# The first 18 expert picks are summed between the query tiles of a fused transformer kernel

## The reference, cut to what matters

```python
def chunk(t):
    qh = (t @ w_q).reshape(T, PEER_HEADS, 2, PEER_KEY_DIM // 2)
    s = jnp.einsum('thpd,hpnd->thpn', qh, sub_keys)
    s_top, i_top = lax.top_k(s, PEER_TOPK)
    cand = s_top[:, :, 0, :, None] + s_top[:, :, 1, None, :]
    cand_idx = i_top[:, :, 0, :, None] * PEER_N_KEYS + i_top[:, :, 1, None, :]
    best, pos = lax.top_k(cand.reshape(T, PEER_HEADS, 256), PEER_TOPK)
    idx = jnp.take_along_axis(cand_idx.reshape(...), pos, axis=-1)
    g = jax.nn.softmax(best, axis=-1)
    ue = jnp.take(u_tab, idx, axis=0)
    ve = jnp.take(v_tab, idx, axis=0)
    act = jax.nn.gelu(jnp.einsum('thkd,td->thk', ue, t), approximate=False)
    return jnp.einsum('thk,thkd->td', g * act, ve)
```

## Time and profile before

| what | value |
|---|---|
| time, median of 3 runs | 3190.19 us (3185.8 to 3191.19) |
| span of the profiled execution, first to last instruction | 3170.1 us |
| busy in the span: PE, DVE, ACT, POOL | 87%, 67%, 40%, 20% |
| mean granted TensorE clock | 0.941 of full speed |
| HBM read | 784.05 MB |
| bytes fetched by index | 536.90 MB, 73728 packets |
| indices of unit 0 ready, first fetch | 577.7, 578.75 us |
| last query tile done, first dot | 613.3, 619.17 us |

### The profile page before, as it was taken

The page is one execution under the profiler, slowest core; times in us unless marked ns, Lnnn a source line. Parts: engine busy times, 40 slices in busy tenths (PEclk is TensorE's granted clock), DMA queues, the critical chain, the costliest instruction groups (busy, mean ns, idle before and its releaser), DMA issues. The chain is left out here.

```text
span 3170.1 us, 39855 instructions
## 1 busy us (share of the span) xinstructions
PE 2755.9 (87%) x13380; PEld 2006.7 (63%) x13380; DVE 2135.5 (67%) x4563; ACT 1269.1 (40%) x2848; POOL 625.3 (20%) x531
## 2 busy tenths in 40 slices
PE   6999898887789887588888999597888997899998
PEld 6777687633344442245566777365877896778886
DVE  6784454398878876775685666855676778654445
ACT  3336523344434443465453222454543543432222
POOL 0000000244444445333332333230000001000000
PEclk9999899999999999799998999798998998899998
DMA  6531122599999999899898999883322453222221
GB/s 236 214 123 61 41 80 81 212 421 421 421 421 420 420 416 414 318 364 417 348 407 351 396 417 417 348 351 140 127 87 87 160 188 111 87 93 93 93 93 53
DMA packets 145015, 788.52 MB, mean 249 GB/s; under 512 B 15297, under 2 KB 18497, under 8 KB 79041
## 3 DMA queue, kind: packets, MB, share of 16 engines
q0 software_dynamic: 73728, 536.90, 41.4%
q1 hardware_dynamic: 65424, 229.90, 20.3%
q10 hardware_dynamic: 5680, 19.40, 1.7%
HBM read 784.05 MB, written 2.10 MB: 248 GB/s over the span
## 5 line engine op out<-in xcount | busy, mean ns | idle before, releaser
L581 POOL DMA_INDIRECT slots<-in_experts,consts x312 | 374.1, 1199 | 1189.5 <-DVE consts L2148 577.9
L2171 DVE SCALAR_TENSOR_TENSOR slots<-slots,work 128x1024 f32<-128x1024 f32 x312 | 382.1, 1225 | 93.0 <-DMA slots<-in_experts,consts 80.8
L883 PE MATMUL psum<-slots,acc 128*128 128x512 f32 x652 | 317.9, 631 | 77.0 <-ACT acc L1482 77.0
L1796 DVE TENSOR_TENSOR wlo<-w,whi 128x1024 fp32r<-128x1024 f32 x259 | 314.5, 1220 | 84.2 <-ACT whi L1277 83.5
L1277 ACT ACTIVATE whi<-w 128x1024 fp32r<-128x1024 f32 x259 | 272.3, 1053 | 215.8 <-PE psum L629 210.0
L883 PEld LDWEIGHTS psum<-slots,acc 128*128 128x128 f32 x652 | 124.8, 200 | 255.7 <-issue 131.4
L627 PE MATMUL psum<-xhi,whi 128*128 128x512 f32 x632 | 255.3, 404 | 1.9 <-DVE wlo L1796 1.9
L628 PE MATMUL psum<-xlo,whi 128*128 128x512 f32 x632 | 250.5, 396 | 0.0
L629 PE MATMUL psum<-xhi,wlo 128*128 128x512 f32 x632 | 250.5, 396 | 0.0
L1470 ACT ACTIVATE consts<-consts 128x1 f32<-128x1 f32 x512 | 101.0, 197 | 360.2 <-DVE slots L2171 215.7
L614 PE MATMUL psum<-xres,w 128*128 128x256 f32 x1040 | 238.3, 386 | 0.0
(11 more groups left out here) (358 smaller groups left out, 5829.5 us busy)
## 6 DMA issues: line engine op xcount, KB each, us to landing
w<-in_stream SPq DMA_DIRECT2D x408, 512.0 KB, 3.6
arena<-in_wmod SPq DMA_DIRECT2D x4, 2048.0 KB, 17.8
arena<-in_wmod ACTq DMA_DIRECT2D x8, 1024.0 KB, 5.5
acc<-in_wmod ACTq DMA_DIRECT2D x8, 1024.0 KB, 8.1
slots<-in_experts,consts POOLq DMA_INDIRECT x312, 17.1
split_slots<-in_experts,consts POOLq DMA_INDIRECT x148, 17.8
xres<-in_xT SPq DMA_DIRECT2D x1, 2048.0 KB, 14.8
outT<-xres SPq DMA_DIRECT2D x8, 256.0 KB, 2.0
```

The lines of the kernel that those rows point to most:

```text
L581: pool.indirect_dma_start(out=slots[slot], out_offset=None, in_=a["experts"], in_offset=bass.IndirectOffsetOnAxis(ap=indices[:, p:p + 1], ...
L883: mm = pe.matmul(bank(6 + half), diag(p), v[:, half * T:(half + 1) * T], start=(c == 0), stop=(c == PICKS - 1))
L1796: dve.tensor_tensor(wlo[:, s, :, :].rearrange("p k n -> p (k n)"), w32[:, s, :], whi[:, s, :, :].rearrange("p k n -> p (k n)").bitcast(F32 ...
L2171: dve.scalar_tensor_tensor(u, u, 1.0, tokens[:, p // PICKS, :], ALU.mult, ALU.mult, accum_out=inner[:, c:c + 1]).then_inc(sem("dotted"), 1)
```

## The change

- DVE runs the search of unit 0 through (keys, pairs, experts) with one weight split in between, and does the later splits behind it. ACT's exponential for unit 0 moves from behind the query tiles into step 7.
- Picks 0 to 17 are taken up behind query tiles 9 to 15: 3, 2, 3, 2, 3, 2, 3 of them (`SUMMED_BY`). In a step DVE does the dots ahead of its split, ACT the weights behind its copies and its split, PE the sums behind the scores.
- Until pick 22 only the six slots 4, 5, 7, 8, 10, 11 are used; the eight others open at pick 22 (`SLOTS_OPEN`).
- So that banks 6 and 7 are free for the sums, the scores of tiles 8 to 15 go to bank 4 (`key_bank`). The diagonals of the first 18 picks and the identity for turning the tokens lie in constants that are not used there; slots 10 and 11 move to offset 8192 and wait for two token copies instead of eight. All other edits are counts that follow from this. No pick below 336 is added by DVE (`on_dve`).

```diff
+QUERY_PICKS = 18
+SUMMED_BY = {9: 3, 10: 5, 11: 8, 12: 10, 13: 13, 14: 15, 15: 18}
+SLOTS_OPEN = QUERY_PICKS + 4
-    free, slots = [4, 5, 7, 8, 10, 11, 0, 1, 2, 3, 12, 13, 14, 15], []
+    free, slots = [4, 5, 7, 8, 10, 11], []
     for p in range(NPICKS):
+        if p == SLOTS_OPEN:
+            free = [0, 1, 2, 3, 12, 13, 14, 15] + free
...
+        def key_bank(m):
+            return 6 if m < 8 else 4
...
                 elif q is None and slot == 10:
-                    pool.wait_ge(sem("tokens_copied"), 2 * TT)
+                    pool.wait_ge(sem("tokens_copied"), 2)
...
             for m in range(4, HP):
                 linear(n + m, o + m)
                 key_scores(m - 1)
                 if m < 8:
                     turn_tokens(m - 4)
+                for p in range(SUMMED_BY.get(m - 1, 0), SUMMED_BY.get(m, 0)):
+                    expert_sum(p)
             key_scores(HP - 1)
...
-            for p in range(EARLY):
+            for p in range(QUERY_PICKS, EARLY):
                 expert_sum(p)
...
+            for m in range(HP):
+                if m >= 2:
+                    act.wait_ge(sem("key_scores"), m - 1)
+                copy_product(acc[:, m % 2, :], o + m)
+                if m:
+                    scores_copy(m - 1)
+                if 5 <= m < 9:
+                    tokens_copy(m - 5)
+                upper_after(n + m)
+                if m == 7:
+                    gates_exp(0)
+                for p in range(SUMMED_BY.get(m - 1, 0), SUMMED_BY.get(m, 0)):
+                    expert_weight(p)
...
             top_keys(0, 0)
             top_keys(0, 1)
-            lower_after(n + 5)
-            lower_after(n + 6)
             top_pairs(0, 0)
             top_pairs(0, 1)
-            lower_after(n + 7)
-            lower_after(n + 8)
+            lower_after(n + 5)
             pick_experts(0, 0)
             pick_experts(0, 1)
-            for m in range(9, 16):
+            lower_after(n + 6)
+            lower_after(n + 7)
+            pick_gates(0)
+            lower_after(n + 8)
+            for m in range(9, HP):
+                for p in range(SUMMED_BY.get(m - 1, 0), SUMMED_BY[m]):
+                    expert_dot(p)
                 lower_after(n + m)
-            pick_gates(0)
-            for p in range(EARLY):
+            for p in range(QUERY_PICKS, EARLY):
                 expert_dot(p)
```

More of the change, by code:

```diff
@@ L365, in build @@
         slots = [slots_all[:, j, :] for j in range(6)] + [flat_acc[:, 2048:4096]] + [slots_all[:, j, :] for j in (6, 7)]
-        slots += [ar(6144, 2 * D), ar(8320, 2 * D), ar(8320 + 2 * D, 2 * D)]
+        slots += [ar(6144, 2 * D), ar(8192, 2 * D), ar(8192 + 2 * D, 2 * D)]
         slots += [split_slots[:, j, :] for j in range(4)]
@@ L839, in key_scores @@
                     pe.wait_ge(sem("key_scores_copied"), m)
+                if m == 8:
+                    pe.wait_ge(sem("tokens_copied"), 2 * TT)
                 for t in range(TT):
-                    mm = pe.matmul(bank(6)[:, t * P:(t + 1) * P], acc[:, m % 2, t * P:(t + 1) * P], sub_keys[:, m, :],
+                    mm = pe.matmul(bank(key_bank(m))[:, t * P:(t + 1) * P], acc[:, m % 2, t * P:(t + 1) * P], sub_keys[:, m, :],
                                    start=True, stop=True)
@@ L857, in turn_tokens @@
                     mm.then_inc(sem("tokens_turned"), 1)
[L859 to L867, removed]
             def expert_sum(p):
@@ L875, in expert_sum @@
                 t, c = p // PICKS, p % PICKS
-                if c == 0:
-                    pe.wait_ge(sem("peer_added"), 8 * t) if t else pe.wait_ge(sem("tokens_copied"), 2 * TT)
+                if on_dve(p):
+                    return
+                if c == 0 and t:
+                    pe.wait_ge(sem("peer_added"), 8 * t)
                 if p == 0:
-                    pe.wait_ge(sem("key_scores_copied"), HP)
-                pe.wait_ge(sem("diagonal"), p + 1)
+                    pe.wait_ge(sem("key_scores_copied"), 8)
+                pe.wait_ge(sem("diagonal"), ON_PE[p] + 1)
                 v = slots[SLOT[p]][:, D:2 * D]
@@ L930, in turn_copied @@
                 turn_values(src[:, m % 2, :], tiles, bank(at + m % 2))
+            linear_group(n, range(o, o + 4), (sem("split2"), 0))
+            for m in range(3):
+                key_scores(m)
+            for m in range(4, HP):
+                linear(n + m, o + m)
+                key_scores(m - 1)
+                if m < 8:
+                    turn_tokens(m - 4)
+                for p in range(SUMMED_BY.get(m - 1, 0), SUMMED_BY.get(m, 0)):
+                    expert_sum(p)
+            key_scores(HP - 1)
             n, o = SECTIONS["memk"]
-            for p in range(EARLY):
+            for p in range(QUERY_PICKS, EARLY):
                 expert_sum(p)
@@ L1433, in scores_copy @@
                 act.wait_ge(sem("key_scores"), m + 1)
-                act.activation(scores_all[:, :, m, :], bank(6).rearrange("p (t n) -> p t n", t=TT), ACT.Copy)\
+                act.activation(scores_all[:, :, m, :], bank(key_bank(m)).rearrange("p (t n) -> p t n", t=TT), ACT.Copy)\
                     .then_inc(sem("key_scores_copied"), 1)
@@ L1477, in expert_weight @@
                     act.wait_ge(sem("weighed"), p + 1)
-                    if 2 <= p < EARLY:
-                        act.wait_ge(sem("pick_used"), p - 1)
+                    if p < EARLY and ON_PE[p] >= 2:
+                        act.wait_ge(sem("pick_used"), ON_PE[p] - 1)
                     elif p >= EARLY + 4:
@@ L2172, in expert_dot @@
                                          accum_out=inner[:, c:c + 1]).then_inc(sem("dotted"), 1)
-                if p >= EARLY and on_dve(p - ADD_LAG):
+                if p == QUERY_PICKS:
+                    dve.wait_ge(sem("tokens_copied"), 2 * TT)
+                if on_dve(p - ADD_LAG):
                     add_row(p - ADD_LAG)
@@ L2190, in add_row @@
                         dve.wait_ge(sem("peer_turned"), 6)
-                    ins = dve.tensor_scalar(row_sum, row, weights[:, c:c + 1], None, ALU.mult)
+                    ins = dve.tensor_scalar(to, row, weights[:, c:c + 1], None, ALU.mult)
                 else:
                     dve.wait_ge(sem("pick_added"), ON_DVE[p])
-                    ins = dve.scalar_tensor_tensor(row_sum, row, weights[:, c:c + 1], row_sum, ALU.mult, ALU.add)
+                    ins = dve.scalar_tensor_tensor(to, row, weights[:, c:c + 1], to, ALU.mult, ALU.add)
                 ins.then_inc(sem("pick_added"), 1)
```

32 lines of the change are left out of this document (14 added, 18 removed).

## The result

| kernel | time, median | runs | ratio to before, 95% interval |
|---|---|---|---|
| before, beside the change | 3188.04 us | 4 | |
| the change | 3201.45 us (3196.21 to 3209.27) | 4 | 1.0043 [1.0026, 1.006] |

The change makes the kernel slower, by 13.4 us where 16 were forecast. The profiled execution took 3196.21 us and spans 3194.4. The ratios in this document are not quotients of the medians; over all kernels the two differ by up to 0.0018.

A forecast was written before the change was run, and what follows sets the result against it. Expert-pick fetches were taken to set the pace from 613 us to pick 255 near 1290 us. The terms 47.2 - 37.4 + 6 = 15.8, say 16 us slower, gave 3190.2 + 16 = 3206 us, range 3188 to 3219.

The forecast's parts named there:

- The search: Unit 0's search on DVE: keys end at 540.4 us, first fetch at about 554; indices come 24.7 us earlier.
- Hidden splits: DVE's postponed splits, for tile 9 and later: costed at nothing; 1.2 us each if the cover were gone.
- The sums: PE's sums between query tiles: 1.72 us a pick; 16 picks count for the fetches, 27.5 us.
- The pauses: PE waiting for ACT's diagonal ahead of the sums, steps 9 to 15: 19.4 us, bounds 0 and 38.7.
- The clock: PE's clock falling behind pauses: 2.5 falls of 2.41 us, 6 us; bounds 0 and 16.9.
- The slots: Fetch 21 waits for pick 15 on PE; saturated transfers begin there, about 660.8 us, with 21 fetches in hand.
- The signs in the prediction: Expected in the profile: first fetch near 554 us, last query tile's end near 656, fetch 21 near 661.
- The balance: Time transfers become continuous, less 2.49 us per completed fetch: 47.2 us later less 37.4, 9.8 us lost.
- The 20.1 us around the span: Trace span 3170.1 us against timed median 3190.2; the 20.1 between them taken as outside the change.
- The rival of hidden pauses: ACT has diagonals ready when PE leaves the scores: -9.6 us, time 3181; chance 0.13.
- The rival of a delay taken up later: Fetches not the sole bound up to pick 255, late start partly absorbed: 3190 us, give or take 5; chance 0.13.
- The rival of a falling clock in every step: PE's clock falls at each of seven pauses: 9.8 + 16.9 = 27 us slower, time 3217; chance 0.08.

The follow-up runs named there:

- the weights first: The change, with ACT's weights of a step's first two picks ahead of the product's copy and DVE's step 9 dots ahead of the split: 3171.68 us, 0.9943.
- The filled pauses: The change, plus 6 or 10 idle PE matmuls into an unused bank behind the scores in each step: ratio 1.0026.
- five picks: The weights first, with five picks in each of seven steps, 35 by tile 15: 3162.84 us, 0.9924; run again 3167.28 us, 0.9950.
- the search alone: The change with no picks summed between the query tiles and the eight slots opened at pick 6: 0.9985; run again 0.9994.
- the kernel before again: The kernel before the change, unedited, timed and profiled a second time: 3186.25 us, ratio 1.0002.
- the placement only: The search alone, but with DVE's and ACT's order from before the change; the moved places are kept: ratio 1.0008.
- three blocks: The change with its 18 picks in three blocks of six, behind tiles 11, 13 and 15: ratio 1.0002.

## Why the prediction was right

The direction, the cause and nearly the size were right. That 15.8 us lies between the 13.4 timed and the 16.8 seen is in part luck, since two terms were off in opposite directions: the pauses 1.0 us too high, the clock 2.3 us too low. By its own steps, measured from A where that is 2.8 us later than in the trace of before:

- **The search.** Forecast 13.6 us from the end of the keys to the first fetch (540.4 to 554); measured 556.70 - 543.22 = 13.5. Hidden splits: held, no wait of PE for a split shows in 575 to 675 us, and none of ACT for a dot.
- **The sums.** 1.72 us a pick: in the kernel with the weights first, a step of three picks is 591.30 - 579.66 = 11.64 us from scores to scores. 6.49 + 3 x 1.72 = 11.65.
- **The pauses.** Forecast 19.4 us; counted in the same way (from the scores' start + 0.80 us to the first sum) they are 4.31, 2.74, 2.73, 1.79, 3.21, 1.79, 1.79 = 18.4. Single ones are up to 0.27 shorter: the split holds ACT 0.94 us before the Gelu, not 1.05, and from Gelu to matmul it is 1.01 (596.77 to 597.78), not 1.17. That they are the mechanism is shown by the weights first, which took them away and turned +16.8 into -8.6.
- **The clock.** This term was mis-sized: 6 us forecast, 8.3 measured. Each step less the same step of the kernel with the weights first, less the delay of its first sum against that kernel (0.09 us less than the pauses above), gives 1.5, 1.8, 1.8, 0.1, 3.0, 0.1 and 0.1 us. Four falls, not two and a half, of 2.0 us on average, not 2.41. The windows agree: a mean clock of 0.90 over the 86 us from 575 to 661 us is, as an estimate, 8.6 us of work lost at half speed. The falls go with the pause's length more strictly than the mLSTM's one in three made me think: none behind 1.54 us, all four behind 2.48 and more. By the Trainium skill, "TensorE: Matmul & The Clock Gate", section "Part 1: The HAM clock gate", the slow clock is the resting state and only sustained activity lifts it. Read as a fall behind each pause, that held for those four and not for the three short ones. The filled pauses bear the size out: 7.6 us back in Z - A.
- **The slots.** Fetch 21 is the hinge, as forecast: released by pick 15's sum, then no more long waits. 94.1 us behind A against 86.6 forecast without the clock and 92.6 with it. Of the 1.5 left, 2.3 are the clock, -1.0 the pauses, and 0.2 stay unexplained. The signs in the prediction left the clock's 6 us out: the last query tile's end was to be near 656 us and fetch 21 near 661; the scores behind tile 15 start at 665.88 and fetch 21 goes out at 671.00, 7 us later beyond A's 2.8.
- **The balance.** Worked +17.4 with what S measured, seen +16.8, forecast +15.8. It is the part that carried all experiments. The timed difference, 13.4 us, is lower; its interval (0.26% to 0.6%, 8 to 19 us) holds all of them.
- **The 20.1 us around the span** were wrong as a reading. In the change's trace the span and the time of the same execution differ by 1.8 us. A second trace of before spans 3190.8 us, 20.7 more than the first: the first was a short execution, 16.4 us shorter behind Z and 4.9 ahead of A. It did no harm, since the sum was added to the median.

The rival of hidden pauses needs a total pause under 9.6 us. The change didn't meet that, and the weights first and five picks did: for 18 picks -9.6 was its forecast, -8.6 is seen. The rival of a delay taken up later falls: Z - A moves one for one with the balance, and from 700 us on share and GB/s are as before. The rival of a falling clock in every step (27 us) is out too: four of seven.

**Open.** The timed differences (of the medians) lie on average some 4 us below the seen ones over the nine series with picks in the query tiles, the most with the weights first: -16.2 us timed, -8.6 seen. The two series of the search alone lie 7.4 and 3.5 us below as well, and the two with the old order of the search don't (the kernel before again at 0.0, the placement only 3.5 above). Singly most of these lie within the 4 to 6 us of their intervals, but the eleven series with the early search all point one way. So it may be worth a few us outside of the stretch from A to Z; no run isolates that. From Z to the end, the traces scatter from 1873.5 to 1895.4 us, those of one and the same kernel too (before: 1874.0 and 1890.4), so a single trace can't tell whether something behind Z gains a few us or whether it is chance. The same kernel with five picks measured 0.9924 and 0.9950, further apart than either half width of about 0.0018.

## What to carry to other kernels

Where a queue of transfers sets the pace, add up two things only: when the transfers become continuous, and how many are in hand by then. Work that feeds the stream earlier pays its time on the engine that opens the slots, so look at what the engine that feeds it does just before, in its own order: here the same 18 picks lost 17 us with ACT's short weights behind its copies and won 9 with them ahead. And group the pauses that you can't avoid: three blocks lost a third of what seven did.

## What was unexpected of the hardware

- **Longer pauses were followed by falls of the clock more often.** Over the eight traces with pauses of over 1 us ahead of sums among the query tiles (in that with the pauses filled only the one of 1.78 us is left): behind 4.06 us the clock fell 4 times of 4, behind 2.96 us 3 of 3, behind 2.48 us 4 of 6, behind 1.78 to 2.29 us 2 of 4, behind 1.40 and 1.54 us 0 of 15. A fall cost 1.5 to 3.1 us. The length alone doesn't decide: behind the query tiles the clock fell after a pause of 1.70 us in the trace of before (sixteen matmuls from 649.83 us took 9.00, where 7.03 is full speed) and not after one of 2.39 us with the three blocks (eight from 672.71 in 3.70).
- **A table load costs ACT little more than its row.** Steps with a load have pauses 1.57 and 1.42 us longer than their like without; the row shows 1.28.
- **Single executions scatter by far more than the stretch that matters here:** A lies between 574.2 and 579.7 us over all traces, Z to the end between 1873.5 and 1895.4, while Z - A of the five traces without picks in the query tiles lies within 1.0 us (721.3 to 722.3).
